# Mixture-of-experts kernel: gathering and computing expert 0's first block ahead of the index table

## What is computed

```python
def hmoe(x, w_rg, b_rg, w_re, b_re, w_g, w_u, w_d):
    gp = softmax(x @ w_rg + b_rg)                  # 4 groups, the best one is taken
    g_idx = argmax(gp)
    el = take(einsum('nd,gde->nge', x, w_re) + b_re, g_idx)   # its 8 experts
    top_v, top_i = top_k(el, 2)                    # the best two
    wts = softmax(top_v) * g_p
    eid = g_idx * 8 + top_i                        # 2 * 640 pairs (token, expert), 32 experts
    ...
    hid = silu(xblk @ w_g[e]) * (xblk @ w_u[e])    # 1024 -> 512
    yb = hid @ w_d[e]                              # 512 -> 1024
    y = segment_sum(yb * row_w)                    # back to the tokens

x = x + g2 * y
```

## Time and profile before

| | us |
|---|---|
| median of 3 executions | 1784.78 (1784.57 to 1785.18) |
| the profiled execution, whole | 1786.67 |
| its span, first to last instruction | 1784.5 |
| PE busy | 1550.3 (87%) |
| DVE busy | 616.7 (35%) |
| ACT busy | 249.2 (14%) |
| POOL busy | 247.2 (14%) |
| DMA, mean over the span | 299 GB/s |

### The profile page before, as it was taken

One profiled execution on the slowest core, in us unless ns is written; L12 is line 12 of the kernel. 1 busy time (PEld: TensorE's weight loads), 2 busy tenths in 40 slices (PEclk: granted clock), 3 DMA queues, 4 the chain that ended last, 5 costly groups with the idle time before them and its releaser, 6 DMA issues.

```text
span 1784.5 us, 19903 instructions
## 1 busy us (share of the span) xinstructions
PE 1550.3 (87%) x6788; PEld 715.9 (40%) x6788; DVE 616.7 (35%) x1194; ACT 249.2 (14%) x497; POOL 247.2 (14%) x376
## 2 busy tenths in 40 slices
PE   4999897789999999888884799999899999898881
PEld 2445444545433333333332344545433333333330
DVE  2499645743622222122123320233622222212224
ACT  2110023621100000000002111011100000000001
POOL 0024020000112111111110001000121121121110
PEclk9899998999999999999997899999999999999996
DMA  9754233041699999999997654252899999999995
GB/s 345 262 175 174 97 140 154 25 154 45 233 415 418 419 419 420 420 420 420 421 418 288 222 196 142 95 236 75 310 418 420 417 418 419 420 420 420 419 421 225
DMA packets 118640, 534.15 MB, mean 299 GB/s; under 512 B 18185, under 2 KB 19010, under 8 KB 68138
## 3 DMA queue, kind: packets, MB, share of 16 engines
q1 hardware_dynamic: 96016, 493.46, 68.9%
q0 software_dynamic: 12032, 21.08, 3.2%
q10 hardware_dynamic: 10522, 18.64, 3.0%
HBM read 522.55 MB, written 27.33 MB: 308 GB/s over the span
## 4 chain that ended last, share of the span: by engine, by line
PE 38%; SPq 19%; DMA 15%; DVE 4%; issue 3%; ACT 2%; ACTq 0%; POOLq 0%; DVEq 0%
SPq L497 18%; PE psum_pair_B L1775 12%; DMA scratch<-w_up 8%; PE psum_pair_C L1797 7%; PE psum_pair_B L1666 4%; PE psum_pair_A L1666 4%; DMA weight_ring<-w_up 3%; PE psum_pair_C L1713 3%; PE psum_pair_D L1713 3%; DMA scratch<-modulation_rows 1%; DMA weight_ring<-w_ada 1%; PE psum_pair_C L1607 1%; PE psum_pair_D L1784 1%; PE psum_pair_D L1706 1%; DVE scratch L1351 1%
## 5 line engine op out<-in xcount | busy, mean ns | idle before, releaser
L1775 PE MATMUL psum_pair_B<-weight_ring,gates_by_token 128*64 128x512 f32 x1408 | 313.5, 594 | 25.4 <-DMA weight_ring<-w_up 21.8
L1775 PE MATMUL psum_pair_B<-scratch,gates_by_token 128*64 128x512 f32 x896 | 199.3, 593 | 11.4 <-DMA scratch<-w_up 11.4
L1351 DVE TENSOR_TENSOR scratch<-psum_pair_B,scratch 128x256 f32<-128x256 f32 x72 | 30.6, 424 | 507.5 <-ACT scratch L884 507.5
L1775 PEld LDWEIGHTS psum_pair_B<-weight_ring,gates_by_token 128*64 128x64 f32 x1408 | 112.5, 137 | 218.8 <-issue 194.2
L1797 PE MATMUL psum_pair_C<-weight_ring,scratch 128*64 128x512 f32 x704 | 160.8, 597 | 25.0 <-issue 22.6
L692 POOL DMA_INDIRECT expert_rows<-scratch,scatter_rows x72 | 73.4, 1019 | 717.7 <-DVE scratch L1363 717.7
L1666 PE MATMUL psum_pair_A<-scratch,weight_ring 128*128 128x128 f32 (+1 forms) x512 | 146.4, 444 | 4.4 <-DVE scratch L1402 2.8
L884 ACT ACTIVATE scratch<-psum_pair_B 128x256 f32<-128x256 f32 x72 | 27.6, 383 | 841.9 <-PE psum_pair_B L1775 841.9
L1666 PE MATMUL psum_pair_B<-scratch,weight_ring 128*128 128x128 f32 (+1 forms) x512 | 142.2, 436 | 0.0
L1775 PEld LDWEIGHTS psum_pair_B<-scratch,gates_by_token 128*64 128x64 f32 x896 | 74.7, 137 | 131.5 <-issue 120.2
L1445 DVE SCALAR_TENSOR_TENSOR weight_ring<-weight_ring,params 128x655 f32<-128x655 f32 x120 | 117.1, 976 | 5.0 <-DVE gates_by_token L1093 0.9
(11 more groups left out here) (357 smaller groups left out, 1478.2 us busy)
## 6 DMA issues: line engine op xcount, KB each, us to landing
weight_ring<-w_gate SPq DMA_DIRECT2D x88, 1024.0 KB, 27.2
weight_ring<-w_up SPq DMA_DIRECT2D x88, 1024.0 KB, 28.2
weight_ring<-w_down SPq DMA_DIRECT2D x88, 1024.0 KB, 28.1
weight_ring<-w_ada SPq DMA_DIRECT2D x24, 2048.0 KB, 8.7
scratch<-w_up SPq DMA_DIRECT2D x40, 1024.0 KB, 27.9
scratch<-w_down SPq DMA_DIRECT2D x40, 1024.0 KB, 27.6
scratch<-w_gate SPq DMA_DIRECT2D x40, 1024.0 KB, 26.6
weight_ring<-w_in_e SPq DMA_DIRECT2D x5, 2048.0 KB, 14.5
```

The lines of the kernel that those rows point to most:

```text
L1351: tt(HID[par], PB[B_][:, 512 * par + 256:512 * par + 512], SIL[par], ALU.mult).then_inc(sig("hidden", l), 1)
L1775: ins = mm(PB[B_][CAP * q:CAP * (q + 1), 512 * par:512 * par + 512].rearrange("p (u n) -> p u n", u=2), XGT[par][:, at:at + CAP], w[:, :, ...
```

## The change

It has these parts, the same in both layers:

1. Right after the ranks, VectorE makes a one-hot `HOT0` of the seats of expert 0 alone (5 tiles x 64 seats) and TensorE multiplies it with the token numbers (`first`). VectorE turns the result into `GI[0]`, and GpSimd gathers block 0 from it. Before, block 0's gather needed the whole table.
2. The index table is made in two parts inside block 0: five products after the gate and up products with k = 5, five after the last; then the weights table, then `turn_hidden`, and only then `turn_rows` of block 1. Seven of the 13 `keep_busy` calls behind the ranks are gone (six are left: two before `first` and four behind it).
3. `ORD` is worked out in two parts: places 3 to 8 before the one-hots, places 9 to 31 while block 0's down products run, in the memory of `H2[1]`. The numbers of further blocks follow after block 0's output.
4. SP no longer waits for `weights` before it waits for `order_known`. The first and second halves of gate and up of the expert at place 3 are issued first, and then the scratch slot's page of expert 2.
5. ScalarE stores the last tile's rows first, does its two exponentials, and then issues the four loads of `G2`; its first SiLU waits for `row_weights` as well.

The diff, cut to its core (in the part of VectorE's `experts`, the body of a block is only split into `hidden`, `gates` and `rows_out`):

```diff
--- before.py
+++ after.py
+        HOT0 = scr(2560 - NT * CAP, NT * CAP).rearrange("p (t c) -> p t c", t=NT)
+        LATE = SQ[:, 516:516 + D]
...
-            put(C_, "rank", l), put(D_, "table", l), put(D_, "weights", l)
+            put(C_, "rank", l), put(D_, "first", l), put(D_, "table", l), put(D_, "weights", l)
...
-                def expert(pos, st, done):
+                def expert(pos, st, done, scratch_page=False):
...
                     load(e, st, 1, (1,))
+                    if scratch_page:
+                        page_free(sp, ("weights", l))
+                        load(2, 2, 0)
...
-                page_free(sp, ("weights", l))
-                load(2, 2, 0)
-                sp.wait_ge(sig("order_known"), l + 1)
+                sp.wait_ge(sig("order_known"), 2 * l + 1)
                 for pos in range(3, 9):
-                    expert(pos, pos % 3, done_with(pos - 3))
+                    expert(pos, pos % 3, done_with(pos - 3), pos == 3)
+                sp.wait_ge(sig("order_known"), 2 * l + 2)
...
-                sp.wait_ge(sig("routed"), l + 1)
+                sp.wait_ge(sig("scatters_counted"), l + 1)
...
+                gathered = [sig("gathered", l, i) for i in range(2)]
+                scattered = [sig("scattered", l, i) for i in range(2)]
+                pool.wait_ge(sig("h2_stored", 0), 48 * (l + 1))
+                pool.wait_ge(sig("h2_stored", 1), 32 * (l + 1))
+                after(pool, "first", l)
+                pool.indirect_dma_start(XG[0], None, h2_dram, bass.IndirectOffsetOnAxis(GI[0][:, :], 0),
+                                        bounds_check=2 * TOK - 1, oob_is_err=False).then_inc(gathered[0], 16)
                 pool.wait_ge(sig("block_of_pair"), 2 * (l + 1))
                 pool.tensor_tensor(VAL[:, 1], EQ, rows_flat[1].unsqueeze(2).broadcast_to([128, 10, NBLK]), ALU.mult).then_inc(sig("row_values"), 1)
                 after(pool, "table", l)
...
-                for b in range(2):
-                    pool.indirect_dma_start(XG[b], None, h2_dram, bass.IndirectOffsetOnAxis(IDX[:, b:b + 1], 0),
-                                            bounds_check=2 * TOK - 1, oob_is_err=False).then_inc(gathered[b], 16)
+                pool.indirect_dma_start(XG[1], None, h2_dram, bass.IndirectOffsetOnAxis(IDX[:, 1:2], 0),
+                                        bounds_check=2 * TOK - 1, oob_is_err=False).then_inc(gathered[1], 16)
...
+                stored(NT - 1)
+                act.wait_ge(sig("router_z"), 2 * l + 1)
+                act.activation(scr(RT + 0, 20), scr(RT + 0, 20), ACT.Exp).then_inc(sig("router_exp"), 1)
+                act.wait_ge(sig("router_z"), 2 * l + 2)
+                act.activation(scr(RT + 20, 5), scr(RT + 20, 5), ACT.Exp).then_inc(sig("router_exp"), 1)
                 take(act, "lg", l, NT - 2)
                 for c in range(2):
                     for h in range(2):
                         row = mod_dram[l, c, 5 * D + h * 512:5 * D + (h + 1) * 512]
                         act.dma_start(G2[CAP * h:CAP * (h + 1), c], row.partition_broadcast(CAP)).then_inc(sig("rows_back", 5), 16)
...
+                act.wait_ge(sig("row_weights"), l + 1)
                 body(0, 0, False)
...
+                seat0 = tmp(NT)
+                link(stt(seat0, p[:, 0:NT * NE:NE], 1.0, CHB[:, 0:NT * NE:NE], ALU.add, ALU.mult))
+                stt(HOT0, iota["c"].unsqueeze(1).broadcast_to([128, NT, CAP]), 1.0, seat0.unsqueeze(2).broadcast_to([128, NT, CAP]),
+                    ALU.add, ALU.is_equal).then_inc(sig("first_hot"), 1)
...
+                f = take(dve, "first", l)
+                took(ts(GI[0][:, :], f[:, 60:61], HALFROW, None, ALU.add), "first", l)
...
+                def order_of(places, room, order):
+                    n = places.stop - places.start
+                    of_place = room[:, 0:n * NE].rearrange("p (a b) -> p a b", a=n)
+                    link(tt(of_place, place.unsqueeze(1).broadcast_to([128, n, NE]), iota["s"][:, places].unsqueeze(2).broadcast_to([128, n, NE]), ALU.is_equal))
+                    link(tt(of_place, of_place, iota["E"].unsqueeze(1).broadcast_to([128, n, NE]), ALU.mult))
+                    link(dve.tensor_reduce(order[:, 0:n], of_place, AX_X, ALU.add))
+                    dve.tensor_copy(ORD[:, places], order[:, 0:n]).then_inc(sig("order_known"), 1)
+
+                order_of(slice(3, 9), pairs.rearrange("p k x -> p (k x)"), code)
...
+                order = tmp(NE, where="near")
+
+                def later_places():
+                    dve.wait_ge(sig("h2_stored", 1), 32 * (l + 1))
+                    order_of(slice(9, NE), LATE, order)
+
+                def further_blocks():
...
+                hidden(0, 0)
+                slot_table(l)
                 dve.wait_ge(sig("rows_back", 5), 64 * (l + 1))
-                slot_table(l)
-                body(0, 0, None)
+                gates(0, 0)
+                later_places()
+                rows_out(0, 0, None)
+                further_blocks()
...
-                keep_busy(10)
-                p = fill(pe, "table", l)
-                for i in range(10):
-                    pe.wait_ge(sig("one_hots"), 2 * l + i // 5 + 1)
+                keep_busy(2)
+                pe.wait_ge(sig("first_hot"), l + 1)
+                p = fill(pe, "first", l)
+                for t in range(NT):
+                    for h in range(2):
+                        ins = mm(p[CAP * h:CAP * (h + 1), 60:61], HOT0[:, t, :], ROWS[:, 0, 0, t:t + 1], start=(t == 0), stop=(t == NT - 1))
+                filled(ins, "first", l)
+                keep_busy(4)
+
+            def index_table(l, part):
+
+                p = PB[D_] if part else fill(pe, "table", l)
+                pe.wait_ge(sig("one_hots"), 2 * l + part + 1)
+                for i in range(5 * part, 5 * part + 5):
                     ins = mm(p[:, 0:NBLK], POSH[:, i, :], VAL[:, 0, i, :], start=(i == 0), stop=(i == 9))
-                filled(ins, "table", l)
-                keep_busy(1)
+                if part:
+                    filled(ins, "table", l)
+
+            def weights_table(l):
+
                 p = fill(pe, "weights", l)
                 pe.wait_ge(sig("row_weights"), l + 1)
                 for i in range(10):
                     ins = mm(p[:, 768:768 + 2 * NBLK].rearrange("p (s b) -> p s b", s=2), POSH[:, i, :], VAL[:, 1:3, i, :], start=(i == 0), stop=(i == 9))
                 filled(ins, "weights", l)
-                keep_busy(2)
...
                         if k == 3:
                             ins.then_inc(sig("gate_up_half", l), 1)
+                        if type(b) is int and b == 0 and k == 5:
+                            index_table(l, 0)
...
                     gate_up(b, par, st, first, nth)
-                    if not last:
-                        turn_rows(b + 1, 1 - par, rows, first and par == 0)
-                    turn_hidden(b, par)
+                    if type(b) is int and b == 0:
+                        index_table(l, 1)
+                        weights_table(l)
+                        turn_hidden(b, par)
+                        turn_rows(b + 1, 1 - par, rows, True)
+                    else:
+                        if not last:
+                            turn_rows(b + 1, 1 - par, rows)
+                        turn_hidden(b, par)
```

65 lines of the change are left out of this document (26 added, 39 removed).

## The result

| | before | after |
|---|---|---|
| median | 1784.57 us (13 executions, 1779.87 to 1790.04) | 1791.43 us (13 executions, 1788.92 to 1800.04) |
| ratio after / before | | 1.0043, interval 1.0029 to 1.0057 |
| the same once more, on another occasion | 1786.42 us (19 executions) | 1790.93 us (12), 1.0027, interval 1.0016 to 1.0038 |
| span of the profiled execution | 1784.5 | 1789.6 |

The change made the kernel slower, by 6.9 us at first and by 4.5 us on the other occasion. I had said 1784.3, within 1777.5 to 1789.5. It is outside, on the side of rival C.

What follows compares the result with a forecast made beforehand. Bound: the stream of pages in the expert stage, PE mattering only through what it frees. Layer 0 +1.5 and layer 1 -1.0 sum to 0.5 us gained, carried over to the median: 1784.3 us, range 1777.5 to 1789.5.

Steps and rivals of the forecast that it cites:

- rival C: Both layers: slow block 1 gather, clock falls at both idles, late first gather in layer 1; 4.1 to 6 us lost, 25%.
- The bound: Expert stage: its end is set by when the page stream became continuous and bytes moved until then, at 419 GB/s.
- `first` taken as 2.0 us: Layer 0, block 0: the 20 PE instructions take 2.0 us, between 1.3 and 2.6, done at 466.9.
- The start of the stream in layer 0: Half pages issued at 477.3 us instead of the scratch page at 479.7, so the stream starts 2.4 us earlier.
- the rival that it comes late: VectorE's longer chain brings the order after 477.3, half pages slip one for one; 3 us of room, part of C (25%).
- Block 1's gather: Layer 0: runs among the second half pages, takes 6.5 us, lands at 490.8; PE idles 3.5 us before it.
- The hole ahead of the down page: Layer 0: pages are moved by 496.1, the down page flows from 497.2; 1.1 us lost.
- the fall of the clock: PE idle ahead of block 0's and block 1's transposes: each fall costs 1.5 us or nothing; one counted per layer.
- Layer 0 in sum: Stream gains 2.4 + 1.7 - 1.1 = 3.0 us, less 1.5 for the clock: +1.5 us gained.
- Layer 1, the step that failed: Layer 0's 3.0 us less 2.5 for block 0's gather under load gives 0.5, with one clock fall -1.0 us.
- The stored rows: Layer 1: block 0's gather waits for the last tile's rows, taken as there by 1264; if late, up to 4 us lost.
- Rival B: Both layers: clock holds (3.5 us gained), or block 1's gather also lands like an unloaded one (8.2); about 1779 us, 33%.

Runs made afterwards that it cites:

- the page behind the gather: Changed kernel with expert 1's down page issued only once block 0's gather has landed, both layers; 1784.52 us, 0.9986 to the kernel before.
- the experiment with the scratch page: Changed kernel with the scratch slot's page issued before expert 3's half pages again; 1800.23 us, 1.0079 to the kernel before.

## Why the prediction was wrong, point by point

- **The bound.** Right. A gather that was issued 3.4 us later made layer 0's stage 3.6 us longer, and the bytes of the first 60 us give the lengths nearly everywhere.
- **`first` taken as 2.0 us.** Too dear: 0.75, below my lower bound of 1.3. Products started 9.0 us after the ranks; my 473.4 is 10.7 after the 462.7 of before. Of the 1.7 us between them 1.1 lie ahead of the end of `first`, and the gather took 3.1 us to the transposes where before it took 4.1.
- **The start of the stream in layer 0.** Half pages at 12.9 us after the ranks (my 477.3 is 14.6), a gain of 4.1 instead of 2.4. The order was there in time, so the rival that it comes late falls.
- **Block 1's gather.** 6.4 us against my 6.5. The wait of PE was there, 3.6 us against 3.5.
- **The hole ahead of the down page.** I had 1.1 us for it and 1.5 for the fall of the clock, 2.6 together; measured 3.4. I let the down products end where they ended before; the fall cost 2.1 in them and 0.4 in the transposes, and the first half page flowed sooner, so the queue ran dry sooner. The experiment with the down products first puts the whole place of block 1's gather at 4.4 us, close to the 3.4 and 0.9 us that the windows of layer 0 show lost.
- **Layer 0 in sum.** +1.5 predicted, 1.3 measured, and that they fit is luck. The start was better by 1.7; the hole with the fall was 0.8 longer; and from 488 to 496 us, where I had the stream at its full rate, 0.9 us were lost. That leaves 0.2 unassigned.
- **Layer 1, the step that failed.** "So layer 1 gains 3.0 - 2.5 = 0.5, and with one fall of the clock -1.0, ..." That puts layer 1 2.5 us below layer 0 (-1.0 against +1.5). Measured it is 7.1 below (-5.8 against +1.3). Two terms make the difference. (1) The first gather under load: I took 2.5 us more than an idle one; it took 4.2 more than layer 0's, since I compared it with the 4.35 of the earlier trace rows, while layer 0's new gather took 3.1 to the transposes. My own row of a gather under load, 7.3, was the right size, and I used it for block 1 alone. (2) I counted one fall of the clock in each layer. Layer 1 had two: 0.4 + 1.9 ahead of block 0, which layer 0 doesn't have, and 0.4 + 1.8 ahead of block 1, as in layer 0. So 4.2 + 2.3 = 6.5 of the 7.1 us are found on PE, and block 0's products came 4.5 us later than layer 0's where I had named 2 to 3 as the sign. The experiments bear it out: with the page behind the gather both terms go and the stage is 6.6 us shorter. With filling products the clock alone is kept, and 1.0 us goes, so the gather is the larger of the two. The last 0.6 us are not assigned.
- **Rival C.** Its mechanism is the one that happened (first gather of layer 1 late, PE's place ahead of block 1's gather decides, clock falls), with 1788.9 to 1790.8, a little under the 1791.4 measured. It had 25%, and its layer 1 (-3.3, -5 with late rows) was still too mild, its layer 0 (-0.8) too hard. The point that I gave for it, down products that end 3 us later than before, was met in layer 0 by the clock of the profile (498.5 against 495.4); from the ranks they end 0.3 later, and the layer still gained. That point was a wrong measure, as the experiment with the scratch page shows. The stored rows, its worst case, were no hindrance.
- **Rival B.** Block 1's gather did not land like an unloaded one. The Trainium skill's figure (DMA: Bandwidth & Descriptors, "Anatomy of one DMA — SWDGE (gpsimd) path") is an estimate of 2.6 us; layer 0's first gathers, with the DMA engines nearly idle, took 2.8 to 3.3 us from issue to transposes here, a little above it and below my 3.7. With pages under way a gather took 6.4 to 7.9, and there the figure doesn't hold. The Trainium skill's turns between queues, in the same title's section "Queues, rings and completion order", would explain that; no run here shows the turns themselves.
